# First feed-forward pass: GpSimd multiplies half of ctx's first modulation tiles, ScalarE adds them up, and VectorE's gates stand ahead of its weight rests

## The chip, the cores and the metric

The kernel runs as one program on one core of a Trainium2 chip. The metric is the device time of that core in microseconds, taken over several executions. One execution is recorded by the hardware profiler, and every row below comes from it.

## The reference, cut to what matters

Two transformer-like blocks of two layers each are applied to x, 256 tokens of width 1024. In the first block a second stream, ctx (also 256 tokens), goes along. Every sublayer of that block is modulated by nine vectors a layer that depend on a condition alone: c for x, c_ctx for ctx.

```python
silu_c, silu_cc = jax.nn.silu(c), jax.nn.silu(c_ctx)
mx = (silu_c @ ada_w[i] + ada_b[i]).reshape(B, N_MOD, 1, D)
mc = (silu_cc @ ada_w[i] + ada_b[i]).reshape(N_MOD, D)
hx = _ffn_sublayer(hx, (mx[:, 0], mx[:, 1], mx[:, 2]), g[0], g[1], ffn_w_in[i, 0], ffn_w_out[i, 0])
hc = _ffn_sublayer(hc, (mc[0], mc[1], mc[2]), g[0], g[1], ffn_w_in[i, 0], ffn_w_out[i, 0])
# _ffn_sublayer: u = rmsnorm(h) * (1 + scale) + shift; a, b = split(u @ w_in); y = (silu(a) * b) @ w_out
```

What the change touches is the shift and scale vector of the very first sublayer (m = 0 and 1 of layer 0) for ctx, and the order of work around the first matmuls of the first sublayer for x.

## The kernel before, in words

The five engines run hand-written instruction streams that wait for one another by semaphores. There is no scheduler: the order of the calls is the order on the engine.

**Weights.** Each weight slot (128 x 2048 float32, 1 MB) is loaded by SyncE into a ring of three (`w_raw`). ScalarE copies it to a rounded high part (`make_high`, L344, called through `highs(g)`: all slots up to g), VectorE subtracts the high part from it to get the rest (`make_rest`, L354, through `rests(g)`). TensorE multiplies twice with the high part (L370, L371) and once with the rest (L851 in this pass). A slot is loaded again when the rest of the slot three before it has been made.

**First pass.** Features are worked in 11 groups f; group f has two weight slots (the halves of the contraction). For x the first six slots go in the order 0, 1, 2 (first halves of f = 0, 1, 2) and 3, 4, 5 (their second halves), each slot for two token halves tt. The second halves need the second half of the modulated input (`u_parts`), which comes from `take_first(1)` (L417 to L420: shift and scale of x), `first_shift_dve(1)` (L735), `first_part_act(1)` (L721, L726) and `first_part_dve(1)` (L744). After group f's two halves ScalarE takes the silu (L998), VectorE multiplies by the gate (L1006), TensorE turns the product (`turn_gate`, L923: the wait of TensorE on `gate_done`), ScalarE makes its high part (L1016) and VectorE its rest (L1026). `turn_gate(f - 1)` stands in TensorE's stream behind slot 4 (f = 1), slot 5 (f = 2) and slot 6 (f = 3).

**Modulation sums.** A modulation vector is a matrix-vector product that VectorE makes from rows: `sum_first(tile, c, n)` (L409) multiplies a 128 x 1024 tile of `ada_w` by the condition row (`cond_rows`, both in SBUF) and adds up along the row, in one instruction and a small read of the accumulator. The first sublayer's 16 tiles (`ada_first`, the last two in `ada_tiles`) are summed 16 times for x in the opening and then 16 times for ctx in between the gates (`sums_of_ctx(f)`, three a time by the table FIRST_CTX). The count of these sums is the semaphore `ada_used`. The condition rows pass through a silu on ScalarE (`silu_cond`, L2835) first; ScalarE must have loaded the silu table for it. The ctx sums have to be done before the part of the buffer that holds their tile is overwritten by the gated results.

**GpSimd** has no work in this pass. Its first work is `na_bias` (L2013) in mixer 4: 32 instructions on 128 x 256 that take two SBUF operands, without a wait between them. From mixer 10 on it takes taps of a convolution (L2378, L2382).

## Time and profile before

| what | value |
|---|---|
| median of 3 runs | 2838.33 us (2836.46 to 2840.06) |
| the profiled execution | 2836.42 us, span from first to last instruction 2834.6 us |
| TensorE busy in the span | 2753.5 us, 97% |
| VectorE, ScalarE, GpSimd busy | 2057.4 us (73%), 1607.1 us (57%), 136.0 us (5%) |
| TensorE's waits from 26 us to 160 us of the span | 6.1 us before its first matmul of the pass, 3.5 us in three waits on the gates |

Times in the rows are microseconds from the start of the span. Busy times overlap between engines; what counts for the kernel's time is a wait of the engine that is nearly always busy.

### The profile page before, as it was taken

How to read it: one execution, taken by the hardware profiler on the slowest of the kernel's cores; microseconds unless marked ns; L12 is line 12 of the kernel's file. 1: busy time of each engine (PE TensorE's matmuls, PEld its weight loads, DVE VectorE, ACT ScalarE, POOL GpSimd, SP SyncE). 2: the span in 40 equal slices, each digit the busy share in tenths (PEclk: the TensorE clock that was granted, in tenths of full speed). 3: DMA queues.
4: the chain of work that ended last, by engine and by line, in shares of the span. 5: the costliest groups of instructions: out<-in, count | busy, mean ns of one | idle time of the engine just before them, and what ended most of it. 6: DMA issues, size and time to landing. Idle time of an engine off the chain costs nothing.

```text
span 2834.6 us, 37737 instructions
## 1 busy us (share of the span) xinstructions
PE 2753.5 (97%) x14816; PEld 2328.5 (82%) x14816; DVE 2057.4 (73%) x2637; ACT 1607.1 (57%) x2413; POOL 136.0 (5%) x140
## 2 busy tenths in 40 slices
PE   6999999989999999999999999999899999998999
PEld 5888878768888888888887788887688888896887
DVE  7879886777879878788746665665666565697664
ACT  5455556686555555555646654554855454476553
POOL 0000000000000000000030000000000000194000
PEclk9999999999999999999999999999999999999999
DMA  8677685307677677678652455554355565550553
GB/s 340 216 218 288 240 254 177 112 3 264 225 245 256 240 224 252 234 258 297 228 213 94 140 188 191 195 191 163 142 194 193 178 208 193 177 174 7 212 181 132
DMA packets 100561, 562.72 MB, mean 199 GB/s; under 512 B 20256, under 2 KB 20768, under 8 KB 43936
## 3 DMA queue, kind: packets, MB, share of 16 engines
q1 hardware_dynamic: 100384, 560.30, 57.2%
q8 instruction: 118, 1.93, 0.3%
q14 instruction: 59, 0.48, 0.0%
HBM read 559.17 MB, written 1.09 MB: 198 GB/s over the span
## 4 chain that ended last, share of the span: by engine, by line
PE 80%; DVE 7%; ACT 4%; DMA 3%; issue 3%; POOL 3%; SPq 0%; DVEq 0%; ACTq 0%; POOLq 0%
PE banks L877 23%; PE banks L883 12%; PE banks L370 9%; PE banks L371 9%; PE banks L1051 8%; PE banks L375 3%; PE banks L377 3%; PE banks L376 3%; DVE w_rest L354 2%; DVE ada_terms L451 2%; PE banks L851 2%; POOL od_glu L2382 2%; POOL normed L2378 1%; ACT w_high L344 1%; DMA w_raw<-in_w_ffn_in 1%
## 5 line engine op out<-in xcount | busy, mean ns | idle before, releaser
L354 DVE TENSOR_TENSOR w_rest<-w_raw,w_high 128x2048 fp32r<-128x2048 f32 x426 | 979.8, 2301 | 469.8 <-ACT w_high L344 469.0
L344 ACT ACTIVATE w_high<-w_raw 128x2048 fp32r<-128x2048 f32 x426 | 811.5, 1908 | 359.4 <-PE banks L1051 162.1
L877 PE MATMUL banks<-u_parts,w_high 128*128 128x512 f32 x3200 | 764.1, 391 | 0.0
L877 PEld LDWEIGHTS banks<-u_parts,w_high 128*128 128x128 f32 x3200 | 588.3, 188 | 114.2
L883 PEld LDWEIGHTS banks<-u_parts,w_rest 128*128 128x128 f32 x3200 | 410.3, 191 | 15.6
L883 PE MATMUL banks<-u_parts,w_rest 128*128 128x256 f32 x3200 | 415.1, 283 | 0.0
L370 PE MATMUL banks<-w_high,gated_high 128*128 128x512 f32 x968 | 377.9, 390 | 0.0
L371 PE MATMUL banks<-w_high,gated_rest 128*128 128x512 f32 x968 | 376.8, 389 | 0.0
L451 DVE CUSTOM_DVE_ANT_0 ada_terms<-ada_tiles,cond_rows 128x1024 f32<-128x1024 f32 x224 | 273.7, 1222 | 8.3 <-DMA ada_tiles<-in_w_ada 2.6
L1051 PE MATMUL banks<-w_rest,gated_high 128*128 128x512 f32 x968 | 258.9, 389 | 1.1 <-DVE w_rest L354 1.1
L1051 PEld LDWEIGHTS banks<-w_rest,gated_high 128*128 128x128 f32 x968 | 181.6, 188 | 39.1 <-DVE w_rest L354 1.5
L370 PEld LDWEIGHTS banks<-w_high,gated_high 128*128 128x128 f32 x968 | 181.8, 188 | 37.2 <-ACT w_high L344 0.2
L371 PEld LDWEIGHTS banks<-w_high,gated_rest 128*128 128x128 f32 x968 | 181.8, 188 | 37.0
L375 PE MATMUL banks<-u_parts,w_high 128*128 128x256 f32 (+1 forms) x544 | 175.9, 323 | 0.0
L377 PE MATMUL banks<-u_parts,w_rest 128*128 128x256 f32 (+1 forms) x544 | 175.0, 322 | 0.0
L376 PE MATMUL banks<-u_parts,w_high 128*128 128x256 f32 (+1 forms) x544 | 175.0, 322 | 0.0
L949 ACT ACTIVATE silu_out<-banks 128x512 f32<-128x512 f32 x100 | 59.3, 593 | 194.2 <-PE banks L883 194.2
L963 ACT ACTIVATE silu_out<-silu_out 128x512 f32<-128x512 f32 x100 | 63.0, 630 | 127.5 <-DVE silu_out L957 127.5
L370 PE MATMUL banks<-w_high,u_parts 128*128 128x512 f32 x288 | 114.5, 398 | 6.1 <-DVE u_parts L744 6.1
L371 PE MATMUL banks<-w_high,u_parts 128*128 128x512 f32 x288 | 113.3, 393 | 0.0
L375 PEld LDWEIGHTS banks<-u_parts,w_high 128*128 128x128 f32 x544 | 104.3, 192 | 10.6 <-issue 3.0
L376 PEld LDWEIGHTS banks<-u_parts,w_high 128*128 128x128 f32 x544 | 104.2, 192 | 7.6
(307 smaller groups left out, 3328.3 us busy)
## 6 DMA issues: line engine op xcount, KB each, us to landing
w_raw<-in_w_ffn_in SPq DMA_DIRECT2D x242, 1024.0 KB, 5.0
w_raw<-in_w_ffn_out SPq DMA_DIRECT2D x121, 1024.0 KB, 5.0
ada_tiles<-in_w_ada SPq DMA_DIRECT2D x128, 512.0 KB, 4.5
w_raw<-in_w_mix SPq DMA_DIRECT2D x54, 1024.0 KB, 5.1
w_raw<-in_w_mix_out SPq DMA_DIRECT2D x22, 1024.0 KB, 5.0
ada_first<-in_w_ada SPq DMA_DIRECT2D x7, 1024.0 KB, 15.0
post_gain_row<-post_mod SPq DMA_DIRECT2D x10, 512.0 KB, 7.0
na_bias<-in_na_bias SPq DMA_DIRECT2D x1, 4096.0 KB, 14.2
```

Of the source, the lines that this page charges most:

```text
L344: act.activation(w_high(g)[:, 0:n], raw[:, g % RING, 0:n], ACT.Copy).then_inc(w_hi_ready, 1)
L354: nc.vector.tensor_tensor(w_rest(g)[:, 0:n], raw[:, g % RING, 0:n], w_high(g)[:, 0:n].bitcast(F32), ALU.subtract).then_inc(w_lo_ready, 1)
L370: nc.tensor.matmul(ps, hi_a, hi_b, start=first_, stop=False)
L371: nc.tensor.matmul(ps, lo_a, hi_b, start=False, stop=False)
L375: nc.tensor.matmul(ps, hi_a, hi_b, start=first_, stop=False)
L376: nc.tensor.matmul(ps, hi_a, lo_b, start=False, stop=False)
L377: return nc.tensor.matmul(ps, lo_a, hi_b, start=False, stop=last_)
L451: dve.tensor_tensor_reduce(ada_terms[:], ada_w[:, ada_slot(n)], cond[:, c], 1.0, 0.0, ALU.mult, ALU.add, mod_sum[:, layer * N_MOD + m, c, ...
L877: pe.matmul(ps[n].rearrange("p (a n) -> p a n", a=2), hi[:, w], u[:, c, :, kt], start=kt == 0, stop=False)
L883: ins = pe.matmul(ps[n][:, 0:SEQ], lo[:, w], u[:, c, 0, kt], start=False, stop=kt == KT - 1)
L963: act.activation(fa[:, f % 2], fa[:, f % 2], ACT.Silu).then_inc(silu_done, 2)
L1051: ins = pe.matmul(y_pair(s, c, tt)[:, half], acts_hi(k, tt), w_rest(g)[:, w], start=False, stop=k == 2 * n - 1)
```

## The change

Eight of ctx's sixteen sums leave VectorE. GpSimd multiplies these tiles in place by ctx's condition row (`weigh_ctx_pool`: eight instructions on 128 x 1024, two SBUF operands each, no wait between them), once the sixteenth sum of x is counted and ctx's condition is ready. ScalarE adds each product up along the row with a Copy that has an accumulator output (`fold_ctx_act`), two each in f = 3, 4, 5 and 6 of the first pass. VectorE keeps eight: 3, 2, 1, 1, 1 at f = 0 to 4, and takes ctx's modulation at f = 8.

On ScalarE the silu of ctx's condition row and the load of the silu table stand ahead of the fourth high part (slot 3) and of `first_part_act(1)`; before, they stood behind it. On VectorE the gates of f = 0, 1, 2 stand ahead of the rests of slots 5, 6 and 7; before, behind them.

```diff
-FIRST_CTX = [[14, 15, 0], [5, 1, 6], [7, 2, 8], [3, 9, 4], [10, 11, 12], [13]]
+FIRST_CTX = [[14, 15, 0], [5, 1], [6], [7], [2], [], [], [], []]
+WEIGHED_CTX = [8, 3, 4, 9, 13, 12, 11, 10]
...
         def sums_to(n):
-            return 4 * len(FIRST_PAIRS) + sum(len(a[4]) for a in ada[:n + 1])
+            return 2 * len(FIRST_PAIRS) + sum(len(tiles) for tiles in FIRST_CTX) + sum(len(a[4]) for a in ada[:n + 1])
...
                 sum_first(tile, 1, done + i)
+            nc.vector.wait_ge(ada_used, done + len(FIRST_CTX[f]))
             if f == len(FIRST_CTX) - 1:
+                nc.vector.wait_ge(ctx_folded, len(WEIGHED_CTX))
                 take_mod(0, 1, (1,), -1)
                 take_mod(0, 0, (1,), -1)
+
+        def weigh_ctx_pool():
+
+            pool = nc.gpsimd
+            pool.wait_ge(cond_ready, 2)
+            pool.wait_ge(ada_used, 2 * len(FIRST_PAIRS))
+            for tile in WEIGHED_CTX:
+                rows_of = first_tiles[tile // 2][:, tile % 2]
+                pool.tensor_tensor(rows_of, rows_of, cond[:, 1], ALU.mult).then_inc(ctx_weighed, 1)
+
+        def fold_ctx_act(f):
+
+            act = nc.scalar
+            for n in range(2 * (f - 3), 2 * (f - 2)):
+                tile = WEIGHED_CTX[n]
+                m, kt = FIRST_PAIRS[tile // 2]
+                kt += tile % 2
+                act.wait_ge(ctx_weighed, n + 1)
+                if n:
+                    act.wait_ge(ctx_folded, n)
+                act.activation(junk[:], first_tiles[tile // 2][:, tile % 2], ACT.Copy,
+                               accum_out=mod_sum[:, m, 1, kt:kt + 1]).then_inc(ctx_folded, 1)
+            act.wait_ge(ctx_folded, 2 * (f - 2))
...
         def first_gates_act():
 
-            highs(4)
-            load_table(ACT.Silu)
             highs(5)
...
             rests(4)
             sums_of_ctx(0)
-            rests(5)
             gate_dve(0, 0, 0, 0)
             gate_dve(0, 0, 0, 1)
+            rests(5)
             sums_of_ctx(1)
-            rests(6)
             gate_dve(0, 0, 1, 0)
             gate_dve(0, 0, 1, 1)
+            rests(6)
             sums_of_ctx(2)
             glo_dve(0, 0, 0)
-            rests(7)
             gate_dve(0, 0, 2, 0)
             gate_dve(0, 0, 2, 1)
+            rests(7)
             glo_dve(0, 0, 1)
...
+                if (s, c) == (0, 0) and f < 7:
+                    fold_ctx_act(f)
                 highs(g0 + 2 * f + 1 + LEAD)
                 gates_act(s, c, f)
...
         def _(pool):
+            weigh_ctx_pool()
             mixers[4].pool(pool)
...
             highs(0)
             first_part_act(0)
+            highs(2)
+            load_table(ACT.Silu)
+            silu_cond(1, 1)
             highs(3)
             first_part_act(1)
-            silu_cond(1, 1)
             ffn_act(0, 0)
```

How instructions stand on an engine is shown in three places. First GpSimd, from its constants to its first real work, before:

```order
L3202 MEMSET const-bfloat16-1.0 128x1
L3202 MEMSET const-uint8-127 128x1
L2912 UNCONDITIONAL_BRANCH
L2013 ISA
L2013 TENSOR_TENSOR na_bias<-na_mask,na_bias 128x256 x32
L2400 MEMSET od_glu_padded 128x4x15
```

The same place of GpSimd in the changed kernel (the numbers behind `ada_first` are those of buffers):

```order
L444 TENSOR_TENSOR ada_first_79<-ada_first_79,cond_rows 128x1024
L444 TENSOR_TENSOR ada_first_76<-ada_first_76,cond_rows 128x1024
L444 TENSOR_TENSOR ada_first_77<-ada_first_77,cond_rows 128x1024
L444 TENSOR_TENSOR ada_first_79<-ada_first_79,cond_rows 128x1024
L444 TENSOR_TENSOR ada_first_81<-ada_first_81,cond_rows 128x1024 x2
L444 TENSOR_TENSOR ada_first_80<-ada_first_80,cond_rows 128x1024 x2
L2041 TENSOR_TENSOR na_bias<-na_mask,na_bias 128x256 x32
```

Eight multiplications now stand ahead of everything GpSimd did before.

VectorE's stream from the third sum of f = 0 to the gates of f = 1, before (L409 with `mod_sum 128x1` alone is the read of the accumulator):

```order
L409 ISA ada_terms,mod_sum<-ada_first_75,cond_rows 128x1024
L409 ISA mod_sum 128x1
L354 TENSOR_TENSOR w_rest<-w_raw,w_high 128x2048
L1006 TENSOR_TENSOR gated<-silu_out,banks 128x256 x2
L409 ISA ada_terms,mod_sum<-ada_first_77,cond_rows 128x1024
L409 ISA mod_sum 128x1
L409 ISA ada_terms,mod_sum<-ada_first_75,cond_rows 128x1024
L409 ISA mod_sum 128x1
L409 ISA ada_terms,mod_sum<-ada_first_78,cond_rows 128x1024
L409 ISA mod_sum 128x1
L354 TENSOR_TENSOR w_rest<-w_raw,w_high 128x2048
L1006 TENSOR_TENSOR gated<-silu_out,banks 128x256 x2
```

The same place in the changed kernel:

```order
L412 ISA ada_terms,mod_sum<-ada_first_75,cond_rows 128x1024
L412 ISA mod_sum 128x1
L1034 TENSOR_TENSOR gated<-silu_out,banks 128x256 x2
L357 TENSOR_TENSOR w_rest<-w_raw,w_high 128x2048
L412 ISA ada_terms,mod_sum<-ada_first_77,cond_rows 128x1024
L412 ISA mod_sum 128x1
L412 ISA ada_terms,mod_sum<-ada_first_75,cond_rows 128x1024
L412 ISA mod_sum 128x1
L1034 TENSOR_TENSOR gated<-silu_out,banks 128x256 x2
L357 TENSOR_TENSOR w_rest<-w_raw,w_high 128x2048
```

The gates (L1034) have moved ahead of the rests (L357), and one of three sums between the two pairs of gates is gone. What stands ahead of this place on VectorE, from `take_first(1)` on, is the same in both kernels.

ScalarE's stream from the high part of slots 1 to 3 on, before:

```order
L344 ACTIVATE w_high<-w_raw 128x2048 x3
L721 ACTIVATE normed<-banks,pre_shift,pre_scale 128x128 x4
L726 ACTIVATE u_parts<-normed 128x4x128
L726 ACTIVATE u_parts<-post_term 128x4x128
L2835 ACT_TABLE_LOAD
L2835 ACTIVATE cond_rows<-cond_rows 128x1024
L344 ACTIVATE w_high<-w_raw 128x2048
L297 ACTIVATE table_out<-small 128x1
L344 ACTIVATE w_high<-w_raw 128x2048
```

The same place in the changed kernel:

```order
L347 ACTIVATE w_high<-w_raw 128x2048 x2
L300 ACT_TABLE_LOAD
L300 ACTIVATE table_out<-small 128x1
L2863 ACTIVATE cond_rows<-cond_rows 128x1024
L347 ACTIVATE w_high<-w_raw 128x2048
L749 ACTIVATE normed<-banks,pre_shift,pre_scale 128x128 x4
L754 ACTIVATE u_parts<-normed 128x4x128
L754 ACTIVATE u_parts<-post_term 128x4x128
L347 ACTIVATE w_high<-w_raw 128x2048 x2
```

The table load and the condition's silu moved from behind the second half of `u_parts` to a place ahead of slot 3's high part; there is still one table load.

## Rows read from the trace of the kernel before

**Rows 1.** The page's busy times of the engines over the span.

```profile
PE 2753.5 (97%) x14816; PEld 2328.5 (82%) x14816; DVE 2057.4 (73%) x2637; ACT 1607.1 (57%) x2413; POOL 136.0 (5%) x140
```

**Rows 2.** TensorE's waits from 26 to 160 us: total us, times, longest.

```profile
PE banks L923 <- DVE gated L1006: 3.5, 3, 1.6
```

**Rows 3.** TensorE's timeline: start us, us, what, [idle before, releaser].

```profile
45.37 1.07 PE L851 MATMUL banks<-w_rest,u_parts 128*128 128x512 f32 x4
46.28 0.40 PE L370 MATMUL banks<-w_high,u_parts 128*128 128x512 f32 x1
...
56.28 1.07 PE L851 MATMUL banks<-w_rest,u_parts 128*128 128x512 f32 x4
58.99 0.66 PE L923 MATMUL banks<-identity,gated 128*128 128x128 f32 x4 [1.65 <-DVE gated L1006]
...
65.76 0.66 PE L923 MATMUL banks<-identity,gated 128*128 128x128 f32 x4 [0.63 <-DVE gated L1006]
...
73.12 0.66 PE L923 MATMUL banks<-identity,gated 128*128 128x128 f32 x4 [1.25 <-DVE gated L1006]
```

**Rows 4.** VectorE's timeline from 41 us: small ops, second half of the input, ctx's sums.

```profile
41.52 0.16 DVE L420 SCALAR_TENSOR_TENSOR pre_scale<-mod_sum,params 128x4 f32<-128x4 f32 x1
41.79 1.37 DVE L735 TENSOR_SCALAR post_term<-banks,pre_scale,pre_shift 128x128 f32<-128x128 f32 x4
43.07 2.28 DVE L354 TENSOR_TENSOR w_rest<-w_raw,w_high 128x2048 fp32r<-128x2048 f32 x1
45.27 0.69 DVE L744 TENSOR_TENSOR u_parts<-normed,u_parts 128x512 fp32r<-128x512 f32 x1
...
52.08 1.22 DVE L409 CUSTOM_DVE_ANT_0 ada_terms<-ada_tiles,cond_rows 128x1024 f32<-128x1024 f32 x1
...
53.46 1.23 DVE L409 CUSTOM_DVE_ANT_0 ada_terms<-ada_tiles,cond_rows 128x1024 f32<-128x1024 f32 x1
```

**Rows 5.** ScalarE's timeline from 34 us.

```profile
34.67 1.92 ACT L344 ACTIVATE w_high<-w_raw 128x2048 fp32r<-128x2048 f32 x1 [5.68 <-DMA w_raw<-in_w_ffn_in]
41.10 1.92 ACT L344 ACTIVATE w_high<-w_raw 128x2048 fp32r<-128x2048 f32 x1 [4.51 <-DMA w_raw<-in_w_ffn_in]
...
45.61 1.28 ACT L2835 ACT_TABLE_LOAD   x1
46.91 1.06 ACT L2835 ACTIVATE cond_rows<-cond_rows 128x1024 f32<-128x1024 f32 x1
```

**Rows 6.** SyncE's timeline: the issue of ctx's condition row.

```profile
18.61 2.47 SPq L2838 DMA_DIRECT2D cond_rows<-in_cond  x1
```

**Rows 7.** The tile `cond_rows` to 60 us: its two loads' times to landing.

```profile
DMA to landing us min/median/max: 4.4/12.1/19.9
```

**Rows 8.** Stretch 80 to 100 us: PE, PEld, DVE, ACT, POOL busy; clock, DMA share, GB/s.

```profile
80.00:100.00 20.00, 20.00 (x94) 16.55 (x93) 18.07 (x23) 9.25 (x9) 0.00 (x0) 1.00 0.61 211
```

**Rows 9.** Timelines at `na_bias`: VectorE, and GpSimd's last nine instructions beside it.

```profile
1445.15 2.67 DVE L354 TENSOR_TENSOR w_rest<-w_raw,w_high 128x2048 fp32r<-128x2048 f32 x1 [4.96 <-ACT w_high L344]
...
1455.34 6.29 POOL L2013 TENSOR_TENSOR na_bias<-na_mask,na_bias 128x256 f32<-128x256 f32 x9
1456.04 7.75 DVE L354 TENSOR_TENSOR w_rest<-w_raw,w_high 128x2048 fp32r<-128x2048 f32 x1 [8.21 <-ACT w_high L344]
```

**Rows 10.** Timelines in mixer 10: VectorE, and GpSimd beside it.

```profile
2567.57 0.28 DVE L2677 TENSOR_TENSOR od_maps<-od_decays,od_cb_first 128x128 f32<-128x128 f32 x1
...
2569.35 0.68 DVE L2676 TENSOR_TENSOR od_maps<-od_decays,od_cb_first 128x512 f32<-128x512 f32 x1
2569.46 1.16 POOL L2382 TENSOR_TENSOR od_glu<-od_glu,normed 128x256 f32<-128x256 f32 x1
2569.95 0.81 DVE L2677 TENSOR_TENSOR od_maps<-od_decays,od_cb_first 128x128 f32<-128x128 f32 x1
```

**Rows 11.** TensorE's timeline behind a wait in mixer 1.

```profile
414.15 0.50 PE L375 MATMUL banks<-w_high,u_parts 128*128 128x512 f32 x1 [2.09 <-DVE w_rest L354]
```

**Rows 12.** Stretch 415 to 418.5 us, columns as in rows 8.

```profile
415.00:418.50 3.50, 3.50 (x11) 2.63 (x10) 3.11 (x6) 3.50 (x6) 0.00 (x0) 0.55 0.90 301
```

More of the change, by code:

```diff
@@ L241, in build_program @@
         first_mod_ready = sem("first_mod_ready")
+        ctx_weighed = sem("ctx_weighed")
+        ctx_folded = sem("ctx_folded")
         raw_landed = [sem(f"raw_landed{n}") for n in range(RING)]
```

## The prediction

> **What bounds the kernel now.** I read the page first: TensorE is busy 97% of the span [rows 1], so a change counts only by what it adds to or takes from TensorE's waits. Then TensorE's waits in the first pass: 3.5 us in three waits on the gates [rows 2]. TensorE's timeline shows the three, 1.65, 0.63 and 1.25 us [rows 3]. Each is a little more than its bracket. A group of four L851 matmuls moves TensorE on by 0.91 us (45.37 to 46.28), so after the group at 56.28 it was free at 57.19 and the turn began at 58.99: 1.80 us. With 0.15 us more on each of the three the waits are worth **4.0 us**, all that this change can win here. TensorE waits there because VectorE makes three ctx sums and a rest before it gates.
>
> The second thing to see is what stands just ahead. At 46.28 TensorE starts the second halves of the contraction [rows 3]. They need the first L744 of the second half, which ran from 45.27 [rows 4]. Its step is 0.61 us (the next started at 45.88), so it was done about 0.1 us past 45.8, some **0.3 us** before TensorE came. VectorE ran without a gap from L420 at 41.52 to there. A delay of VectorE between 41.3 and 46 us goes to TensorE nearly whole.
>
> The third view is GpSimd beside VectorE, since the change puts GpSimd to work just there. GpSimd's instruction with two SBUF operands of 256 columns takes 6.29/9 = 0.70 us in a back-to-back row [rows 9]. VectorE's rest on 128 x 2048 takes 2.28 us when GpSimd is idle [rows 4]. Beside that row it took 2.67 us once and **7.75 us** once [rows 9]. The latter began at 1456.04 and ended at 1463.79, 2.15 us after GpSimd's last instruction ended (1455.34 + 6.29 = 1461.63): VectorE stood still behind eight GpSimd instructions, then ran its own 2.2 us. In mixer 10 the two take turns: GpSimd's instruction issued at 2569.46 took 1.16 instead of about 0.73 us, held by VectorE's L2676 until about 2569.9. VectorE's next instruction, issued at 2569.95, took 0.81 us against 0.28 when GpSimd is not in its way [rows 10]: held until GpSimd's was done.
>
> So two instructions that both read two SBUF operands exclude each other on these engines. The Trainium skill says the same ("SBUF — State Buffer", section "Who interferes with whom"): the pair of ports is an exclusive lock, the one that starts first keeps it for its whole instruction, and a VectorE instruction with two SBUF inputs contends with GpSimd's reads. By that rule alone VectorE would be held behind one GpSimd instruction at a time. The trace agrees in mixer 10 and disagrees at 1456 us, where one hold went over eight.
>
> **The change part by part.**
>
> *Eight sums leave VectorE.* A sum's step is 53.46 - 52.08 = 1.38 us [rows 4], so VectorE has 11.0 us less to do. In front of the gates of f = 1 one sum goes, in front of those of f = 2 two more. With the gates ahead of the rests (a rest is 2.28 us [rows 4]) the gates of f = 0 come 2.2 us earlier. The silu ahead lets rest 4 come some 2.3 us earlier too: the 1.28 and 1.06 us of the table load and the silu no longer stand ahead of slot 4's high part [rows 5]. The gate of f = 0 needed to be 1.80 us earlier. That is covered 2.5 times, so without any contention all three waits go: **-4.0 us**.
>
> *The silu ahead of slot 3's high part.* Table load and silu take 1.28 + 1.06 = 2.34 us [rows 5]. ScalarE waited there 4.51 us for slot 3 after it had finished slot 2's high part at 36.6 [rows 5]. The condition row was issued at 18.61 [rows 6]; its landing is the longer of the two, 19.9 us, so it lands at 38.5 [rows 7]. The silu ends at 39.6, 1.5 us before slot 3 at 41.10. Cost nothing; if the row landed later than 40 us, each us would go to the second half of the input.
>
> *Gates ahead of rests.* The rests of slots 5 to 7 come 0.7 us later by the gates. TensorE wants a slot's rest only 1.8 us into the slot, behind eight matmuls of the high part (46.28 to 48.1, the same eight as in front of 45.37), and they have over 2 us in hand. Cost nothing.
>
> *Two folds a group on ScalarE.* One is a 1024-column pass (the silu on 1024 took 1.06 us [rows 5]) and an accumulator read and wait, some 1.4 us: 2.8 us a group. In 20 us of this stretch ScalarE is busy 9.25 us [rows 8], a group of 11.4 us of TensorE leaves it 6.1 us. Hidden; the silu of f comes up to 2.7 us later, and TensorE turns it only behind the slot that follows, 5.5 us. Without that cover it would be up to 4 x 2.8 = 11 us.
>
> *Eight multiplications on GpSimd.* No row has this size. Four times the 256-column instruction is 2.8 us, the upper end. If GpSimd's fixed share is like VectorE's, which by 0.69 us at 512 and 2.28 at 2048 columns [rows 4] is 0.16, it is (0.70 - 0.16) x 4 + 0.16 = 2.3 us, the lower end. I take **2.5 us**, 20 us for the eight. On their own nobody waits for them, since the first fold is due near 70 us. The skill's page "GPSIMD Engine Reference", section 3.1, gives 4497 ns for 2048 columns, half of which as an estimate is 2.25 us; by that the sum below would be 1.8 us less.
>
> *What they hold up.* They start with x's sixteenth sum, at 41.3 us, the very moment at which VectorE starts L417 to L420. Every VectorE instruction from there with two SBUF operands (L418, L420, the rest L354, both L744, the sums) meets them; L735 and the gates read PSUM and one SBUF operand and don't. Taking turns, as in mixer 10, VectorE waits once for each of the first instructions. GpSimd 1 until 43.8 holds L418. GpSimd 2 until 46.5 holds L420 to 46.7. L735 (1.3) ends at 48.0. GpSimd 3 until 49.2 holds rest 3, which ends at 51.4. GpSimd 4 until 53.9 holds the first L744: done at 54.5 instead of 45.9. TensorE waits from 46.28 to 54.6. GpSimd 5 puts the second L744 to 57.7, when TensorE has done its first token half. GpSimd 6 puts rest 4 to 60.2 through 62.4, GpSimd 7 and 8 the first two sums to 66.2 and 70.0; the third ends at 71.3, the gates of f = 0 at 71.9. TensorE, through slots 3 and 4 at 66.1, waits again, and begins the turn at 72.0 where it began at 58.99 before: +13.0. From there VectorE is ahead, and the other two waits (0.8 and 1.4) are gone: **+10.8 us**. That holds the -4.0 already.
>
> *The clock.* After a wait of 2.09 us TensorE worked 3.5 us at a granted clock of 0.55 [rows 11, 12], which is mostly the lower level of 1.2 GHz: half of some 3.5 us lost, 1.7 us. The last of two long waits is likely to bring one such stretch: +1.7 us. What the first brings is hidden in the second wait.
>
> **Sum:** 10.8 + 1.7 = +12.5 us. Against the profiled execution (2836.4) that is 2848.9; this execution lies 1.9 us under the median, so the median comes to 2838.3 + 12.5 = **2851 us**. Behind the first pass TensorE stays the bound [rows 1], so nothing gives the loss back.
>
> Bounds of this case: with 2.3 and 2.8 us an instruction +9.2 and +13.3, before the clock. Whether the sums, a custom instruction, are held at all no row shows; if not, the last part shrinks and the sum is +6.2 + 1.7 = +8. So +8 to +15, 2846 to 2853.
>
> **The rivals.**
>
> *VectorE shut out for the whole row of eight*, as at 1456 us. For it: these eight also have no wait between them, and VectorE's L418 comes within 0.1 us of GpSimd's start, as it did at 1456.04. Against it: at 1445.15 the hold was only 0.4 us [rows 9]. Then L418 waits from 41.3 to 61.3, L744 is done at 65.8 (its chain L420, L735, L354, L744 takes 4.5), TensorE waits 19.6 us in one piece, runs slots 3 and 4 (10.9) and turns at 76.8, 17.8 later than before; less 2.2 for the other waits, plus 1.7 to 2.7 for the clock: +18, **2856 us**.
>
> *VectorE is hardly held* (not slower). If VectorE, whose instructions follow each other without a gap, keeps its turn and GpSimd gets only what VectorE leaves, L418 or L420 waits once at most. For it: L2677 at 2567.57 ran its bare 0.28 us in mixer 10 [rows 10]. Against it: GpSimd got its turn at 2569.9 with VectorE's next instruction due [rows 10]. The input's second half slips by about 1.2 us, the waits on the gates still go, the folds come late once: -4.0 + 1 to 3 = -3 to -1, **2836 us**; with no hold at all -4.0, 2834 us. It decides where the holds add up to less than 4.3 us, the 4.0 to be won and the 0.3 in hand: that is two GpSimd instructions.
>
> *The change does nothing*: not possible, the waits on the gates are VectorE's own order, which changes; only as the sum of a small hold and the gain, which is within the case before.
>
> **How the numbers follow.** A measurement of this kernel tells about 0.2%, 5.7 us, from no change. Taking turns 0.50; shut out for the whole row 0.27; hardly held or not at all 0.23. Even the full gain, 4.0 us, is within 0.2%, so nearly all of the last case is "same", with 0.04 for a gain I don't see. Of the first two all but 0.02 (turns, with sums not held and a short instruction) are slower. Faster 0.04, same 0.21, slower 0.75. The likeliest gives 2851 us, its own range 2846 to 2854. The range for 8 in 10 takes in the shut-out case with the upper price, 2858, and most of the third case down to 2836.
>
> **What would show it.** Right: GpSimd's eight at 41 to 61 us or longer, 2.3 to 2.8 us each when unhindered; VectorE's L423, L357 and L772 (the old L420, L354, L744) between 41 and 60 us 2 us or more longer than 0.16, 2.28 and 0.69; a wait of TensorE on L772 of 8 us at 46.3 and one on the gates (L1034) of some 6 us behind it; none at the second and third turn; ScalarE's silu of the condition done before 41.1 us. Wrong: rests of 2.3 us beside a busy GpSimd; a single wait of 20 us would be the first rival, no wait above 1 us at 46.3 the second. The sum would also be wrong if GpSimd's start slipped behind 46 us, or if a later stage gave time back.

## The result, and the profile after

The changed kernel takes **2845.72 us** (median of 11 runs, 2843.44 to 2850.05) against 2838.33 us for the kernel before (11 runs, 2835.79 to 2842.96). The ratio is 1.0029, with a 95% interval of 1.0022 to 1.0037: slower by 6.2 to 10.5 us. The forecast was 2851 us. Of all kernels in this document one execution ran in a slow state (experiment 4's, 4469 us at a mean clock of 0.57); the ratio there leaves it out. The profiled execution has a span of 2841.9 us, 7.3 us more than the span before.

The page's busy times of the changed kernel, to set beside [rows 1]:

```profile
PE 2756.3 (97%) x14816; PEld 2330.7 (82%) x14816; DVE 2062.7 (73%) x2621; ACT 1615.6 (57%) x2429; POOL 162.2 (6%) x148
```

VectorE has eight sums less to do, 11.0 us of work, and yet is busy 5.3 us longer: its instructions have become longer. GpSimd has 26.2 us more. TensorE's waits from 26 to 160 us of the changed kernel, to set beside [rows 2] (total, times, longest; the 11.0 us contain the 6.1 us ahead of the pass's first matmul, which both kernels have):

```profile
PE banks L373 <- DVE u_parts L772: 11.0, 2, 6.1
PE banks L951 <- DVE gated L1034: 4.1, 1, 4.1
```

Three waits on gates have become one, and a wait of 4.9 us on the second half of the input is new. TensorE's timeline shows where, with the turns of f = 0 to 4 (L951), to set beside [rows 3]:

```profile
45.24 1.07 PE L879 MATMUL banks<-w_rest,u_parts 128*128 128x512 f32 x4
51.16 0.77 PE L373 MATMUL banks<-w_high,u_parts 128*128 128x512 f32 x1 [4.86 <-DVE u_parts L772]
...
68.98 1.11 PE L951 MATMUL banks<-identity,gated 128*128 128x128 f32 x4 [4.07 <-DVE gated L1034]
...
77.20 0.60 PE L951 MATMUL banks<-identity,gated 128*128 128x128 f32 x4
...
83.12 0.60 PE L951 MATMUL banks<-identity,gated 128*128 128x128 f32 x4
...
105.84 0.60 PE L951 MATMUL banks<-identity,gated 128*128 128x128 f32 x4
```

The first three turns began at 58.99, 65.76 and 73.12 us before [rows 3]: the changed kernel is 10.0, 11.4 and 10.0 us behind. The turns of f = 3 and 4 came at 84.54 and 95.91 before and come at 94.50 and 105.84 now. From here on I call this last distance, **+9.9 us**, the loss of the first pass; it is free of what the program adds by chance behind it.

VectorE's timeline over the same stretch, to set beside [rows 4]:

```profile
41.30 0.15 DVE L421 TENSOR_TENSOR mod_sum<-mod_sum,params 128x4 f32<-128x4 f32 x1
41.49 2.27 DVE L423 SCALAR_TENSOR_TENSOR pre_scale<-mod_sum,params 128x4 f32<-128x4 f32 x1
43.88 1.37 DVE L763 TENSOR_SCALAR post_term<-banks,pre_scale,pre_shift 128x128 f32<-128x128 f32 x4
45.16 3.10 DVE L357 TENSOR_TENSOR w_rest<-w_raw,w_high 128x2048 fp32r<-128x2048 f32 x1
48.18 2.84 DVE L772 TENSOR_TENSOR u_parts<-normed,u_parts 128x512 fp32r<-128x512 f32 x1
50.94 2.85 DVE L772 TENSOR_TENSOR u_parts<-post_term,u_parts 128x512 fp32r<-128x512 f32 x1
53.71 4.46 DVE L357 TENSOR_TENSOR w_rest<-w_raw,w_high 128x2048 fp32r<-128x2048 f32 x1
58.09 3.42 DVE L412 CUSTOM_DVE_ANT_0 ada_terms<-ada_tiles,cond_rows 128x1024 f32<-128x1024 f32 x1
...
68.17 0.75 DVE L1034 TENSOR_TENSOR gated<-silu_out,banks 128x256 f32<-128x256 f32 x2
```

and GpSimd beside it, one row for each of its first four instructions:

```profile
41.34 2.41 POOL L444 TENSOR_TENSOR ada_first<-ada_first,cond_rows 128x1024 f32<-128x1024 f32 x1 [40.92 <-DVE mod_sum L412]
43.69 2.42 POOL L444 TENSOR_TENSOR ada_first<-ada_first,cond_rows 128x1024 f32<-128x1024 f32 x1
46.05 4.41 POOL L444 TENSOR_TENSOR ada_first<-ada_first,cond_rows 128x1024 f32<-128x1024 f32 x1
50.43 2.81 POOL L444 TENSOR_TENSOR ada_first<-ada_first,cond_rows 128x1024 f32<-128x1024 f32 x1
```

Read the two side by side. L423, an operation on 128 x 4, is issued at 41.49, 0.15 us after GpSimd began, and ends at 43.76, when GpSimd's first instruction does. L763 reads PSUM and runs at its old length. The rest at 45.16 ends at 48.26, 2.2 us behind the end (46.11) of GpSimd's second: it stood until then and ran its own 2.28 us. Meanwhile GpSimd's third was held by that rest: 4.41 us instead of 2.41. The first L772 then waits for the third to end (50.46) and is done about 51.0, and TensorE starts at 51.16. The two engines hold each other by turns.

Counted against the unhindered lengths (0.16, 2.28, 0.69 and 1.22 us, [rows 4]) VectorE is held 2.1 us at L423, 0.8 at rest 3, 2.15 and 2.16 at the two L772, 2.2 at rest 4 and 2.2, 2.0 and 1.9 at the three sums of f = 0: eight holds, **15.5 us**. The whole GpSimd row is one group of the timeline:

```profile
41.34 25.71 POOL L444 TENSOR_TENSOR ada_first<-ada_first,cond_rows 128x1024 f32<-128x1024 f32 x8 [40.92 <-DVE mod_sum L412]
```

It lasts 25.7 us where eight unhindered instructions would take 8 x 2.4 = 19.3.

Last, the stretches behind the two waits, with one further on for comparison (columns as in [rows 8]):

```profile
49.50:56.40 6.90, 5.24 (x12) 4.13 (x13) 6.90 (x3) 0.65 (x1) 6.90 (x4) 0.53 0.36 140
66.50:73.40 6.90, 4.42 (x13) 3.64 (x14) 6.72 (x8) 2.40 (x2) 0.55 (x1) 0.53 0.18 44
80.00:100.00 20.00, 20.00 (x94) 16.55 (x93) 12.99 (x14) 12.14 (x17) 0.00 (x0) 1.00 0.66 240
```

The granted clock is 0.53 over the 6.9 us of each of the two stretches, which begin inside the wait: mostly the lower level, 1.2 GHz. TensorE's next turn came 8.22 us after that of f = 0 (68.98 to 77.20) where an undisturbed one takes 5.92 (77.20 to 83.12), so the second of these stretches cost 2.3 us.

### The profile page after: what moved, and what is told of

The parts are those of the page before. It is cut to its first block, busy times and chain, and to the rows that moved or that the text cites. A ratio compares the mean times of both kernels' runs of the same rounds, so it can differ in the third digit from the quotient of the medians.

```text
span 2841.9 us, 37754 instructions
## 1 busy us (share of the span) xinstructions
PE 2756.3 (97%) x14816; PEld 2330.7 (82%) x14816; DVE 2062.7 (73%) x2621; ACT 1615.6 (57%) x2429; POOL 162.2 (6%) x148
## 4 chain that ended last, share of the span: by engine, by line
PE 86%; DVE 5%; ACT 3%; POOL 3%; DMA 2%; issue 2%; SPq 0%; DVEq 0%; POOLq 0%; ACTq 0%
PE banks L905 26%; PE banks L911 13%; PE banks L373 10%; PE banks L374 10%; PE banks L1079 8%; PE banks L378 3%; PE banks L379 3%; PE banks L380 3%; PE banks L879 2%; POOL od_glu L2410 2%; POOL normed L2406 1%; DMA w_raw<-in_w_ffn_in 1%; DVE w_rest L357 1%; PE banks L701 1%; PE banks L869 1%
## 5 line engine op out<-in xcount | busy, mean ns | idle before, releaser
L357 DVE TENSOR_TENSOR w_rest<-w_raw,w_high 128x2048 fp32r<-128x2048 f32 x426 | 982.9, 2308 | 470.9 <-ACT w_high L347 470.1
L378 PEld LDWEIGHTS banks<-u_parts,w_high 128*128 128x128 f32 x544 | 104.2, 192 | 11.4 <-issue 3.8
```

What stands on the lines that cost most here:

```text
L357: nc.vector.tensor_tensor(w_rest(g)[:, 0:n], raw[:, g % RING, 0:n], w_high(g)[:, 0:n].bitcast(F32), ALU.subtract).then_inc(w_lo_ready, 1)
L378: nc.tensor.matmul(ps, hi_a, hi_b, start=first_, stop=False)
```

## The experiments

The time of one execution varies by 3 to 6 us either way for most kernels here, so each run is read in two ways: its ratio, and the start of the turn of f = 4 in its trace (95.91 before, 105.84 after). Edits are against the changed kernel where nothing else is said.

### 1. The order without GpSimd

```diff
-FIRST_CTX = [[14, 15, 0], [5, 1], [6], [7], [2], [], [], [], []]
+FIRST_CTX = [[14, 15, 0], [5, 1, 6], [7, 2, 8], [3, 9, 4], [10, 11, 12], [13]]
...
-                nc.vector.wait_ge(ctx_folded, len(WEIGHED_CTX))
...
-                if (s, c) == (0, 0) and f < 7:
-                    fold_ctx_act(f)
...
-            weigh_ctx_pool()
```

> The changed order alone: silu ahead of slot 3's high part, gates ahead of rests, but all 16 ctx sums on VectorE in the old table of three at a time; GpSimd and ScalarE's folds have nothing. Turn-taking theory (the loss comes from GpSimd's and VectorE's instructions with two SBUF operands excluding each other): L772 back at 0.69 us, no wait of TensorE at 46 us, the three waits on the gates gone or under 0.5 us in sum: 4 us less than before, 2834 us (2832 to 2836). Rival (the loss comes from the order of VectorE and ScalarE, with the silu ahead of slot 3): 2842 us or more, with the wait at 46 us still there.

Measured: 2835.41 us, ratio 0.9991 (0.9983 to 1.0000); turns of f = 0, 1, 2 at 57.10, 63.00 and 68.93 without a wait, f = 4 at 92.81, 3.1 us ahead of before. One wait on the gates is left, in f = 3:

```profile
81.39 0.66 PE L950 MATMUL banks<-identity,gated 128*128 128x128 f32 x4 [0.93 <-DVE gated L1033]
```

L423 takes 0.16 us and L771 (the L772 of the changed kernel) 0.68. So the silu and the gates ahead win, and what loses is in GpSimd's eight instructions or the folds.

### 2. GpSimd writes and does not read

```diff
-                pool.tensor_tensor(rows_of, rows_of, cond[:, 1], ALU.mult).then_inc(ctx_weighed, 1)
+                pool.memset(rows_of, 0.0).then_inc(ctx_weighed, 1)
```

This kernel leaves out the eight products; everything else, the folds too, is as in the changed kernel.

> GpSimd's eight instructions write zeros over the same tiles (memset, 128 x 1024, estimated 1 us each) instead of multiplying, so ctx's modulation leaves out those eight products; all waits stay. Lock theory (GpSimd's reads exclude VectorE's second SBUF operand): L423, L357 and L772 at their bare 0.16, 2.3 and 0.69 us beside busy GpSimd, TensorE's waits in the first pass gone, 4 us less than before: 2834 us. Rival (any GpSimd instruction that touches SBUF holds VectorE): L423 about 0.9 us, the second half of the input 2 to 3 us late, 2836 to 2838 us.

Measured: 2832.28 us, ratio 0.9982 (0.9973 to 0.9991); the turn of f = 4 at 91.70. VectorE and GpSimd in its timeline:

```profile
41.29 0.95 POOL L444 MEMSET ada_first<- 128x1024 f32 x1 [40.87 <-DVE mod_sum L412]
...
41.47 0.16 DVE L423 SCALAR_TENSOR_TENSOR pre_scale<-mod_sum,params 128x4 f32<-128x4 f32 x1
...
43.11 2.29 DVE L357 TENSOR_TENSOR w_rest<-w_raw,w_high 128x2048 fp32r<-128x2048 f32 x1
```

GpSimd is busy from 41.29 to 48.5 us, beside L423, the rest of slot 3 and both L772, and VectorE is not held for a moment. All waits on the gates are gone: -4.2 us, the whole of the 4.0 us that was to be won, with the folds in place, so these cost TensorE nothing. The products alone are then worth 105.84 - 91.70 = **14.1 us** of loss in the first pass. The Trainium skill ("SBUF — State Buffer", section "Who interferes with whom") says that a VectorE instruction with two SBUF inputs contends with a GpSimd instruction that reads, not with one that only writes; these rows agree.

### 3. The products in quarters

```diff
-                pool.tensor_tensor(rows_of, rows_of, cond[:, 1], ALU.mult).then_inc(ctx_weighed, 1)
+                for n in range(4):
+                    part = slice(256 * n, 256 * n + 256)
+                    ins = pool.tensor_tensor(rows_of[:, part], rows_of[:, part], cond[:, 1, part], ALU.mult)
+                ins.then_inc(ctx_weighed, 1)
```

> Each of GpSimd's eight multiplications is cut into four of 256 columns (32 instructions, 0.70 us each in a row). If a hold lasts one GpSimd instruction, L423, the rests and L772 are held by 0.4 to 0.7 us each instead of 2 us: L772's first is done near 47.5 us, TensorE waits about 1.3 us there, under 1 us on the gates, and turns f = 4 near 93.7 us (before 95.9, changed kernel 105.8); 2835 to 2838 us. Rival (GpSimd's busy time as a whole is what VectorE loses): the same waits as in the changed kernel, 2844 us. Rival (a row of instructions without waits shuts VectorE out, as once at 1456 us): one hold of several us.

Measured: 2833.44 us, ratio 0.9988 (0.9979 to 0.9997); the turn of f = 4 at 93.20. VectorE's and then TensorE's timeline:

```profile
41.51 0.60 DVE L423 SCALAR_TENSOR_TENSOR pre_scale<-mod_sum,params 128x4 f32<-128x4 f32 x1
...
46.26 1.21 DVE L775 TENSOR_TENSOR u_parts<-normed,u_parts 128x512 fp32r<-128x512 f32 x1
...
47.62 0.47 PE L373 MATMUL banks<-w_high,u_parts 128*128 128x512 f32 x1 [1.16 <-DVE u_parts L775]
```

GpSimd does the same arithmetic in 32 instructions, of 0.73 us where nothing is in their way, and each hold on this part of VectorE's chain has shrunk from some 2.1 us to about 0.5. VectorE waits for the rest of one instruction, not for the row. GpSimd pays for it: held by VectorE's instructions again and again, one of its 32 takes 1.71 us in the median and the row lasts from 41.4 to 91.0 us, 49.6 us instead of 25.7. VectorE's holds go on as long, up to 0.6 us each, but TensorE waits for none of the later ones, nor for GpSimd. TensorE's wait falls from 4.9 to 1.2 us, no wait on the gates is left, and the sign of the change turns: 2.7 us ahead of before instead of 9.9 behind.

### 4. One operand in place of two

```diff
-                pool.tensor_tensor(rows_of, rows_of, cond[:, 1], ALU.mult).then_inc(ctx_weighed, 1)
+                pool.tensor_scalar(rows_of, rows_of, 1.0, None, ALU.mult).then_inc(ctx_weighed, 1)
```

GpSimd reads and writes the same eight tiles but leaves out the condition.

> GpSimd's eight multiply their tile by the number 1 instead of by the condition row (one SBUF operand read, 128 x 1024), so ctx's modulation leaves out the condition in eight tiles. If any GpSimd read of SBUF excludes VectorE's two-operand instructions: holds as in the changed kernel (L423 1.5 to 3 us, L772 2 us or more), TensorE's wait at 46 us 3 us or more, 2841 to 2848 us. Rival (it takes two operands on both sides): L423 0.16 and L772 0.69 us as with the writes of zeros, 2834 us.

Measured: 2833.97 us, ratio 0.9987 (0.9978 to 0.9996); the turn of f = 4 at 92.42. VectorE's and GpSimd's timelines:

```profile
41.51 0.93 DVE L423 SCALAR_TENSOR_TENSOR pre_scale<-mod_sum,params 128x4 f32<-128x4 f32 x1
...
43.83 2.28 DVE L357 TENSOR_TENSOR w_rest<-w_raw,w_high 128x2048 fp32r<-128x2048 f32 x1
...
41.39 2.77 POOL L444 TENSOR_SCALAR ada_first<-ada_first 128x1024 f32<-128x1024 f32 x1 [40.97 <-DVE mod_sum L412]
44.13 5.82 POOL L444 TENSOR_SCALAR ada_first<-ada_first 128x1024 f32<-128x1024 f32 x1
```

This run came out by no expectation. The GpSimd instruction is no shorter (2.77 us), but VectorE was held by at most 0.8 us at a time, and in four of eight cases not at all: GpSimd was the one that stood, 5.82 us instead of 2.77. Reading as such does not hold VectorE for a whole instruction, then. The second operand, or the other kind of instruction that comes with it (`tensor_tensor` in place of `tensor_scalar`), is part of it; which and why, no run here tells. The rule named in experiment 2 makes no difference between one operand read and two; these rows do, and they decide.

### 5. Four tiles instead of eight

```diff
-FIRST_CTX = [[14, 15, 0], [5, 1], [6], [7], [2], [], [], [], []]
-WEIGHED_CTX = [8, 3, 4, 9, 13, 12, 11, 10]
+FIRST_CTX = [[14, 15, 0], [5, 1], [6], [7], [2, 10], [11, 12, 13]]
+WEIGHED_CTX = [8, 3, 4, 9]
...
-                if (s, c) == (0, 0) and f < 7:
+                if (s, c) == (0, 0) and f < 5:
```

> GpSimd weighs four tiles instead of eight, ScalarE folds four (f = 3 and 4), VectorE sums twelve (3, 2, 1, 1, 2, 3 for f = 0 to 5). One hold per GpSimd instruction: the first four holds (L423, rest 3, both L772) and the wait at 46 us stay as in the changed kernel (4.9 us and the half clock behind it), rest 4 and the sums of f = 0 are held once at most, so the wait of 4.1 us on the gates of f = 0 falls below 1 us; f = 4 turned near 99.6 us (changed kernel 105.8, before 95.9); 2838 to 2842 us. Rival (the length of the overlap doesn't matter, only that GpSimd is at work): both waits stay.

Measured: 2838.35 us, ratio 1.0004 (0.9996 to 1.0013); the turn of f = 4 at 99.49. GpSimd's four and TensorE's wait:

```profile
41.41 11.89 POOL L444 TENSOR_TENSOR ada_first<-ada_first,cond_rows 128x1024 f32<-128x1024 f32 x4 [40.99 <-DVE mod_sum L412]
...
51.23 0.76 PE L373 MATMUL banks<-w_high,u_parts 128*128 128x512 f32 x1 [4.72 <-DVE u_parts L772]
```

The first wait is unchanged, the second gone: the first four instructions make the wait on the input, the last four that on the gates. TensorE starts the second halves 4.95 us later than before (51.23 against 46.28). The half pace behind that wait, which the second wait covered in the changed kernel, is now paid for: from 51.8 to 56.9 us the matmuls are 0.43 us apart instead of 0.23, and TensorE needs 13.73 us from 51.23 to the turn of f = 0 where experiment 2 needs 10.98 (46.15 to 57.13), 2.8 us more. Less the 4.2 us that the three waits are worth (experiment 2) this makes +3.6.

### 6. The silu back in its old place

```diff
-            highs(2)
-            load_table(ACT.Silu)
-            silu_cond(1, 1)
             highs(3)
             first_part_act(1)
+            load_table(ACT.Silu)
+            silu_cond(1, 1)
```

> The changed kernel with the condition's silu and table load back behind the second half of the input. GpSimd waits for that silu, so it starts near 48 us instead of 41.3. Turn-taking theory: L423, the rest of slot 3 and both L772 unhindered (0.16, 2.3, 0.69 us), TensorE's wait at 46 us gone, but rest 4, the sums and the rests of slots 5 to 7 are held instead, 2.0 to 2.4 us each, eight times in all; waits on the gates and rests add up to some 8 to 12 us by the turn of f = 2, so 2841 to 2848 us. Rival (only the hit on the second half of the input costs; later holds fall in VectorE's slack): 2836 to 2839 us.

Measured: 2849.30 us, ratio 1.0039 (1.0027 to 1.0052). GpSimd starts at 48.15 instead of 41.34, behind the second half of the input: L772 takes 0.69 us, and the wait on it is gone. But the turns wait:

```profile
63.50 1.11 PE L951 MATMUL banks<-identity,gated 128*128 128x128 f32 x4 [6.25 <-DVE gated L1034]
...
74.50 1.12 PE L951 MATMUL banks<-identity,gated 128*128 128x128 f32 x4 [3.47 <-DVE gated L1034]
```

and that of f = 4 comes at 105.72, as late as in the changed kernel (105.84). The loss is not tied to the place at 46 us. From the rest at 49.98 us on VectorE runs without a pause to the gates of f = 0 and f = 1, so that each hold goes on to them. A part of the loss is the silu's own: without work for GpSimd the same move back costs 2.7 us (92.81 in experiment 1, 95.50 with the gates alone in experiment 8). Set against the second of these kernels, the work moved to GpSimd costs 105.72 - 95.50 = 10.2 us here, and 105.84 - 92.81 = 13.0 us in the changed kernel.

### 7. GpSimd behind the gates of f = 0

```diff
             pool.wait_ge(ada_used, 2 * len(FIRST_PAIRS))
+            pool.wait_ge(gate_done, 2)
```

> The changed kernel, but GpSimd also waits for both gates of f = 0, so it starts near 55 us. Turn-taking theory: no wait at 46 us and none at the first turn (57.2 us), then holds of 2.0 to 2.4 us on rests and sums; waits of 1 to 2 us at each of the turns of f = 1 and 2 and in front of the rests of slots 5 to 7: the turn of f = 3 within 3 us of before, 2837 to 2841 us. Rival (only the hit on the second half of the input costs): 2834 us.

Measured: 2842.71 us, ratio 1.0021 (1.0012 to 1.0031); GpSimd at work from 54.9 to 85.7 us. The input and the first turn (57.30) are free, and the waits come at the turns of f = 1, 2 and 3 (two more, 1.6 us together, stand on weight rests), the longest in f = 3:

```profile
88.54 0.66 PE L952 MATMUL banks<-identity,gated 128*128 128x128 f32 x4 [3.46 <-DVE gated L1035]
```

The turn of f = 4 comes at 101.56, 5.7 us behind before and later than was expected. About 1.7 us of it are a half-pace stretch behind this last wait: the next turn comes 13.02 us later instead of 11.35. A later start saves a part of the loss, but does not bring a gain.

### 8. The parts of the order

Three kernels take the order of the stream apart. The first (the silu alone) and the second (the gates alone) are experiment 1 with one half of the reordering undone; the third is the changed kernel with the rests ahead of the gates again.

```diff
             sums_of_ctx(0)
+            rests(5)
             gate_dve(0, 0, 0, 0)
             gate_dve(0, 0, 0, 1)
-            rests(5)
             sums_of_ctx(1)
+            rests(6)
             gate_dve(0, 0, 1, 0)
             gate_dve(0, 0, 1, 1)
-            rests(6)
```

(and in the same way for `rests(7)`; this is the edit of the first and the third. That of the second is the edit of experiment 6.)

> No work for GpSimd, old table of sums, rests ahead of gates as before; only the table load and the condition's silu stand ahead of slot 3's high part. Backlog theory (VectorE's distance to each gate decides): rest 4 comes 2.3 us earlier, so the first wait on the gates (1.8 us) goes, the second shrinks to 0.5 us, the third stays near 1.7 us; f = 4 turned near 94 us (before 95.9, both order changes 92.8): 2 us less than before, 2836 us. Rival (the silu ahead costs by delaying slot 3's high part): a wait at 46 us of 1 us or more.

> No work for GpSimd, old table of sums, silu at its old place; only the gates of f = 0, 1, 2 stand ahead of the rests. Backlog theory: gates of f = 0 done at 56.9 us, no first wait; second wait 0.9 us, third 1.7 us; f = 4 turned near 94.4 us, 1.5 us less than before, 2836.5 us. Rival (the rests, made later, are late for TensorE): a wait of L880 or its like on w_rest of 1 us or more in front of the rests of slots 5 to 7.

> The changed kernel with the rests ahead of the gates again; GpSimd's eight stay. Turn-taking theory: the first wait (4.9 us at 46 us) is unchanged; the rest of slot 5, 2.3 us, stands once more ahead of the gates of f = 0, so their wait grows from 4.1 to 6.3 us and f = 4 is turned near 108 us (changed kernel 105.8); 2847 us. Rival (the order of gates and rests doesn't matter beside the holds): 105.8 us, 2845 us.

Measured: the silu alone 2836.39 us, ratio 0.9995 (0.9986 to 1.0005), f = 4 at 94.10, 1.8 us ahead of before. The gates alone 2834.71 us, 0.9989 (0.9980 to 0.9999), f = 4 at 95.50, 0.4 ahead, with a wait of 0.90 us in f = 3 that I had not expected. Both together win 3.1 (experiment 1), more than the 2.2 of the two apart: either alone leaves waits in f = 1 and f = 2, which the other would have taken away. The rests ahead with GpSimd at work: 2850.12 us, 1.0047 (1.0030 to 1.0063), and

```profile
71.22 1.11 PE L951 MATMUL banks<-identity,gated 128*128 128x128 f32 x4 [6.34 <-DVE gated L1034]
```

The wait grows from 4.1 to 6.3 us, by the one rest that now stands ahead, and f = 4 comes at 108.58, 2.7 us later than in the changed kernel. So the gates ahead are worth 2.7 us with GpSimd at work and 1.3 without (94.10 to 92.81).

### 9. The sums spread over VectorE alone

Experiment 1 with another table: f = 1 and f = 2 have two sums each instead of three, and the three groups behind them take three each.

```diff
-FIRST_CTX = [[14, 15, 0], [5, 1, 6], [7, 2, 8], [3, 9, 4], [10, 11, 12], [13]]
+FIRST_CTX = [[14, 15, 0], [5, 1], [6, 7], [2, 8, 3], [9, 4, 10], [11, 12, 13]]
```

> No work for GpSimd, no folds; silu ahead and gates ahead as in the changed kernel, and the 16 ctx sums on VectorE as 3, 2, 2, 3, 3, 3 for f = 0 to 5. Turn-taking theory: nothing is held, so only VectorE's backlog counts; two sums fewer ahead of the gates of f = 3 than in the order-only kernel take away its last wait (0.9 us): no wait above 0.3 us from 46 to 110 us, f = 4 turned at 91.7 us (order-only: 92.8, before: 95.9), 4 us less than before: 2834 us. Rival (VectorE needs the load taken off by other engines): waits of 1 us or more at f = 3 to 5.

Measured: 2834.76 us, ratio 0.9987 (0.9978 to 0.9996); no wait on any gate, the turn of f = 4 at 91.60, **4.3 us ahead** of before. That is the whole of what could be won in this pass, without GpSimd and without folds, and it beats both the kernel before and the changed one.

### All runs side by side

| kernel | turn of f = 4 against before, us | median against before, us | ratio, 95% |
|---|---|---|---|
| changed kernel | +9.9 | +7.4 | 1.0022 to 1.0037 |
| 1 order only | -3.1 | -2.7 | 0.9983 to 1.0000 |
| 2 writes only | -4.2 | -5.9 | 0.9973 to 0.9991 |
| 3 quarters | -2.7 | -4.3 | 0.9979 to 0.9997 |
| 4 one operand | -3.5 | -3.7 | 0.9978 to 0.9996 |
| 5 four tiles | +3.6 | +0.7 | 0.9996 to 1.0013 |
| 6 silu back | +9.8 | +11.2 | 1.0027 to 1.0052 |
| 7 late start | +5.7 | +4.6 | 1.0012 to 1.0031 |
| 8 silu alone | -1.8 | -1.9 | 0.9986 to 1.0005 |
| 8 gates alone | -0.4 | -3.6 | 0.9980 to 0.9999 |
| 8 rests first | +12.7 | +11.8 | 1.0030 to 1.0063 |
| 9 spread | -4.3 | -2.9 | 0.9978 to 0.9996 |

The median's column is the kernel's median minus that of the kernel before run beside it (2838.33, 2838.14 for 1, 2, 6 and 7, 2837.70 for 3, 4, 5 and 9, 2838.32 for 8). Over all twelve the two columns differ by 3.2 us at most and by -0.9 us on average: what a kernel wins or loses by the turn of f = 4 it keeps to the end, within what these medians can tell.

## Why the prediction was right, and where its sizes were off

The direction, the mechanism and the places were right: the two waits stand where they were put, the other two turns wait no more, and the median lies in the range, 0.3 us below the likeliest case's own range. Point by point:

- **What can be won, 4.0 us.** Right: 4.2 in experiment 2 and 4.3 in 9. From where TensorE could have turned f = 0 to the turn of f = 4 it takes 38.7 us before (57.19 to 95.91) and 34.6 us in both experiments, so the waits and the slower first instructions behind them are worth 4.1 to 4.2; the rest, 0.1 us, is an earlier start.
- **Silu ahead, gates ahead, folds, at no cost.** Right. The silu began at 38.49 (ScalarE's row below) and ended at 39.5 against 39.6 worked out; experiment 2 keeps all three and loses nothing. The fold is 1.05 us and a read of 0.19, some 1.2 us instead of 1.4.

```profile
38.49 1.06 ACT L2863 ACTIVATE cond_rows<-cond_rows 128x1024 f32<-128x1024 f32 x1 [0.40 <-DMA cond_rows<-in_cond]
...
84.25 1.05 ACT L456 ACTIVATE squares_unread<-ada_first 128x1024 bf16<-128x1024 f32 x1
```

- **GpSimd's instruction, 2.5 us.** 2.41 us in the trace, between the 2.3 and 2.8 of the bounds; over four turns the difference makes 0.4 us. The Trainium skill's half of 4497 ns ("GPSIMD Engine Reference", section 3.1), 2.25 us, is 0.16 us short of the trace.
- **Who is held: the term that was mis-sized.** The prediction held L418 by GpSimd 1, L420 by 2, the rest by 3, the first L744 by 4, done at 54.5 with a wait of 8.3 us. In the trace the old L418 (L421, 41.30) had started before GpSimd (41.34) and was not held; the old L420 was held by 1, the rest by the end of 2, the first L744 by 3. One turn less in the chain: done at 51.0, a wait of 4.9 us. The chain behind kept the lead: the turn of f = 0 came at 68.98 instead of 72.0, so **+10.0 us in place of +13.0**.
- **The sums, open in the prediction.** They are held as every other instruction with two SBUF operands: 3.42, 3.18 and 3.13 us against 1.22. The prediction had GpSimd done with the second sum; GpSimd, held itself, worked until 67.05 and held the third as well.
- **The other two waits, -2.2 us.** Right: from +10.0 at the turn of f = 0 the distance goes to +11.4 (2.3 of clock, less 0.8 for the wait that is gone) and back to +10.0 (less 1.4 for the other).
- **The clock, +1.7 us.** 2.3 us in the trace. The first low stretch, behind the wait at 46.3, delayed TensorE too, but inside the second wait, as was said.
- **The sum.** 10.0 - 2.2 + 2.3 = +10.1, against +9.9 in the trace, where the prediction had 13.0 - 2.2 + 1.7 = +12.5. So 3.0 us of the miss are the one turn of the chain; the clock took 0.6 us of that back. The median, +7.4, lies another 2.5 us lower, for which no run here gives a cause (next point): that part of the miss has nothing to do with the mechanism.
- **"Nothing gives the loss back."** Of the profiled pair this was not so: +9.9 at the turn of f = 4, +7.3 at the end. TensorE's waits from 160 to 450 us before, and then in the changed kernel, show a part of the difference:

```profile
PE banks L375 <- DVE w_rest L354: 2.1, 1, 2.1
PE banks L1051 <- DVE w_rest L354: 1.1, 1, 1.1
```

```profile
PE banks L378 <- DVE w_rest L357: 2.0, 1, 2.0
PE banks L378 <- DVE u_parts L735: 0.4, 1, 0.4
```

  The wait of 1.1 us at 215 us is gone, and the half-clock stretch of [rows 12] as well. At 424 us, behind the same wait, the changed kernel has the full clock:

```profile
424.00:427.50 3.50, 3.50 (x22) 2.97 (x21) 3.16 (x4) 3.50 (x4) 0.00 (x0) 1.00 0.66 265
```

  But the difference as a whole is no property of the change. Experiment 6 has the same loss in the first pass, lacks the wait at 215 us too, and its profiled execution ended 13.0 us behind before, 3.2 more than its first pass had lost. The rest of the program adds or takes some 3 us from one execution to the next. The interval of the ratio, +6.2 to +10.5 us, holds the 9.9 of the first pass. The wait at 215 us stands in none of the twelve other traces, and 1.1 us is about the 0.9 by which the medians lie under the turns on average; whether that small part is regularly given back stays open.

**The rivals.** *Shut out for the whole row* is refuted for this stretch: no VectorE instruction was held over more than what was left of one GpSimd instruction, and with quarters the hold became a quarter. But the rest that stood behind eight at 1456 us [rows 9] was no accident of one execution. It comes back at `na_bias` in seven of the thirteen traces, the changed kernel's among them; in the others, such as experiment 1's, the last rest beside the row is hardly held:

```profile
1439.86 28.47 POOL L2041 TENSOR_TENSOR na_bias<-na_mask,na_bias 128x256 f32<-128x256 f32 x32 [1372.81 <-DMA na_mask<-in_na_mask]
1462.95 7.54 DVE L357 TENSOR_TENSOR w_rest<-w_raw,w_high 128x2048 fp32r<-128x2048 f32 x1 [8.43 <-ACT w_high L347]
```

```profile
1428.76 30.54 POOL L2038 TENSOR_TENSOR na_bias<-na_mask,na_bias 128x256 f32<-128x256 f32 x32 [1428.33 <-DMA na_mask<-in_na_mask]
1451.74 2.78 DVE L357 TENSOR_TENSOR w_rest<-w_raw,w_high 128x2048 fp32r<-128x2048 f32 x1 [8.33 <-ACT w_high L347]
```

What tells them apart is when the rest comes. In the seven it came 5.3 to 5.6 us before the row's end and took 7.45 to 7.79 us, that is, it stood until the row was over; in the other six the last one came 7.3 us or more before the end and took 2.5 to 2.8 us. So a VectorE instruction can be shut out for several GpSimd instructions, near the end of that row at least, and taking turns, as in the first pass, is no general rule. Why it happens there and neither with eight instructions of 1024 columns nor with 32 of 256 (experiment 3) stays open; it was not tried by itself. TensorE does not wait for it in the traces of before and after.

*Hardly held* is refuted with two operands of 1024 columns, but it is what happened in experiments 3 and 4. Its rule for the point that decides, holds of less than 4.3 us ahead of the gates, fits: in quarters the eight holds add up to 3.7 us (0.3 to 0.55 each), and most of the gain stood.

## What to carry to other kernels

Work that is moved from VectorE to GpSimd is not free for VectorE when both read two SBUF operands: count a hold of up to one GpSimd instruction for each VectorE instruction that runs beside it (here 15.5 us of holds for 11.0 us of work taken away; at `na_bias` single holds were over 5 us), and look which of those VectorE instructions the busiest engine waits for next. If the work must go to GpSimd, cut it into short instructions; the same arithmetic in quarters turned 9.9 us of loss into 2.7 of gain, though GpSimd then took 49.6 us for it, for which there must be time. And first ask whether the engine is overloaded or only badly ordered: a table that spread the same sums over later groups won all there was.

## What the runs showed of the hardware

- The size of the VectorE instruction does not matter for the hold: one on 128 x 4 took 2.27 us instead of 0.16.
- The hold goes both ways: GpSimd's instruction of 2.4 us took 4.4 beside a rest of 2.3 us, and its row 25.7 us instead of 19.3.
- With one SBUF operand read, GpSimd held VectorE by 0.8 us at most and was itself held, 5.82 us against 2.77; when it only wrote, neither was held (0.95 us each).
- Behind waits of 4.9 and 4.1 us TensorE went on at half pace, 0.43 us from one 512-column matmul to the next instead of 0.23, and behind the waits of 3.5 us in experiments 6 and 7 too; the three waits of before, 1.65 us and less, brought no such stretch.
- The 6.1 us wait ahead of the pass brings one as well, in both kernels: the matmuls are 0.43 us apart from 27.6 to about 32.7 us. The clock column says 1.00 for that time in these two traces, and 0.50 in those of experiments 2 and 9, at the same pace. Where it matters, the distance between matmuls is the surer sign.
- A VectorE rest that came within the last 5.6 us of the `na_bias` row stood until the row's end, 7.45 to 7.79 us instead of 2.3, in seven traces of thirteen.
